# The cross attention's output projection as three products of high and low halves

## The reference

```
def memory_cross_attention(h, m, wq, wk, wv, wo):
    ...
    p = jax.nn.softmax(l, axis=-1).astype(vm.dtype)
    o = jnp.einsum('bhtm,bmhd->bthd', p, vm).reshape(Bn, T, W_X)
    return o @ wo                       # (256 x 256) @ (256 x 1024)
...
x = x + memory_cross_attention(rms_norm(x, norm_x), rms_norm(mem, mem_norm), wq_x, wk_x, wv_x, wo_x)
x = x + hier_moe(rms_norm(x, norm_moe), w_group, b_group, w_router, b_router, w1, w3, w2)
```

## Time and profile before

| | |
|---|---|
| time, median of 3 runs | 673.18 us (672.6 to 673.38) |
| time of the profiled execution | 671.9 us |
| its span, first to last instruction | 670.0 us |
| mean granted PE clock | 0.889 |
| PE busy | 508.9 us (76%) |
| DVE, ACT busy | 205.6 us, 144.5 us |
| DMA | 244.21 MB, 364 GB/s over the span |
| cross attention's output projection, first product to xo3 | 223.5 to 231.3 us |
| first expert product | 240.2 us |

### The profile page before, as it was taken

The page is one execution under the profiler, slowest core; times in us unless marked ns, Lnnn a source line. Parts: engine busy times, 40 slices in busy tenths (PEclk is TensorE's granted clock), DMA queues, the critical chain, the costliest instruction groups (busy, mean ns, idle before and its releaser), DMA issues.

```text
span 670.0 us, 8811 instructions
## 1 busy us (share of the span) xinstructions
PE 508.9 (76%) x3810; PEld 321.5 (48%) x3810; DVE 205.6 (31%) x384; ACT 144.5 (22%) x253; POOL 15.5 (2%) x31
## 2 busy tenths in 40 slices
PE   8999999999999997968743736764483576347575
PEld 7999998999999642413311411331141123114121
DVE  5799565588857431100000100000010000001002
ACT  4764545354635421000000000000000000000002
POOL 1200010001001000000000000000000000000001
PEclk9999999999999999997766978886798879569879
DMA  9998236908798999999999999999999999999994
GB/s 301 388 354 304 77 126 199 374 4 291 251 382 301 421 392 425 429 425 428 427 426 431 425 429 427 425 429 427 429 424 430 427 428 427 425 431 424 425 410 172
DMA packets 48857, 244.21 MB, mean 364 GB/s; under 512 B 6096, under 2 KB 19888, under 8 KB 36912
## 3 DMA queue, kind: packets, MB, share of 16 engines
q1 hardware_dynamic: 48816, 243.62, 90.0%
HBM read 242.53 MB, written 4.22 MB: 368 GB/s over the span
## 4 chain that ended last, share of the span: by engine, by line
PE 53%; DMA 44%; issue 1%; DVE 1%; ACT 1%; POOL 0%; PEld 0%; SPq 0%; POOLq 0%; PEldq 0%; DVEq 0%
PE ps L755 16%; DMA slots_late<-in_w 14%; PE ps L1145 11%; DMA slots_own<-in_w 9%; PE ps L778 7%; DMA attn_data<-in_w 7%; PE ps L1150 6%; DMA slot_last<-in_w 5%; DMA slot_spare<-in_w 5%; DMA slot_mixed<-in_w 5%; PE ps L733 1%; PE ps L826 1%; PE ps L894 1%; PE ps L923 1%; PE ps L1260 1%; PE ps L1008 1%
## 5 line engine op out<-in xcount | busy, mean ns | idle before, releaser
L1145 PE MATMUL ps<-slots_late,x_sb 128*32 128x512 f32 x320 | 85.8, 672 | 36.5 <-DMA slots_late<-in_w 13.4
L1145 PE MATMUL ps<-attn_data,x_sb 128*32 128x512 f32 x160 | 65.0, 719 | 12.4 <-DMA slots_own<-in_w 12.4
L1912 DVE TENSOR_TENSOR slot_extra<-ps,slot_extra 128x512 f32<-128x512 f32 x8 | 5.5, 691 | 214.1 <-ACT slot_extra L1524 214.1
L1145 PE MATMUL ps<-slot_spare,x_sb 128*32 128x512 f32 x128 | 58.8, 658 | 14.7 <-DMA attn_data<-in_w 14.7
L1521 ACT ACTIVATE slot_extra<-ps 128x256 f32<-128x256 f32 x8 | 3.1, 383 | 302.1 <-PE ps L1218 302.1
L1145 PE MATMUL ps<-slots_own,x_sb 128*32 128x512 f32 x240 | 59.4, 691 | 10.3 <-DMA slot_spare<-in_w 3.9
L453 DVE TENSOR_TENSOR w_low<-slots_own,w_high 128x2048 fp32r<-128x2048 f32 (+1 forms) x31 | 62.4, 2014 | 14.9 <-ACT w_high L1330 14.8
L1150 PE MATMUL ps<-slots_own,slot_extra 128*32 128x512 f32 x192 | 48.2, 713 | 16.4 <-DMA slot_last<-in_w 8.2
L1150 PE MATMUL ps<-attn_data,slot_extra 128*32 128x512 f32 x112 | 45.3, 734 | 16.7 <-DMA slots_own<-in_w 16.7
L1330 ACT ACTIVATE w_high<-slots_own 128x2048 fp32r<-128x2048 f32 (+1 forms) x31 | 52.3, 1689 | 17.3 <-PE ps L778 10.8
L755 PE MATMUL ps<-h_high,w_high 128*128 128x256 f32 x224 | 55.4, 288 | 0.0
(11 more groups left out here) (272 smaller groups left out, 880.4 us busy)
## 6 DMA issues: line engine op xcount, KB each, us to landing
slots_own<-in_w SPq DMA_DIRECT2D x24, 2048.0 KB, 34.1
slots_late<-in_w SPq DMA_DIRECT2D x23, 2048.0 KB, 35.0
attn_data<-in_w SPq DMA_DIRECT2D x14, 2048.0 KB, 35.4
slot_last<-in_w SPq DMA_DIRECT2D x9, 2048.0 KB, 35.6
slots_own<-in_w_in SPq DMA_DIRECT2D x8, 2048.0 KB, 10.1
slot_spare<-in_w SPq DMA_DIRECT2D x8, 2048.0 KB, 36.0
slot_mixed<-in_w SPq DMA_DIRECT2D x7, 2048.0 KB, 34.6
attn_data<-in_w SPq DMA_DIRECT2D x6, 1024.0 KB, 9.3
```

The source lines that it names most:

```text
L1145: return pe.matmul(ps[SLOTS * e:SLOTS * e + SLOTS, 4 + matrix, :], xeT[:, k, SLOTS * e:SLOTS * e + SLOTS], w, start=(k == 0), stop=(k == K ...
```

## The change

`xo0` to `xo3` are made of three fp32r products for each of the two depth tiles: high by high, low by high (both with the weights' high half), high by low. That is 24 products of 128x512 where there were 8 in float32.

- ACT makes the high half of wo in three copies (128x1024, 128x512, 128x512), put between its exponentials and before the copy of `vm`. They are written over wv_x, so ACT waits for the split of `vm` first. DVE makes the low half in two subtractions of 128x1024, in place over wo_x.
- ACT's copies of `ox0` and `ox1` now write `ox_high`; DVE subtracts that from PSUM into `ox_low`, and only DVE's instruction frees the bank.
- `xo0` and `xo1` are computed together, depth by depth. PE begins both before the first product.
- Unit 10 has no early half; it is loaded whole when `xo3` is computed.

```diff
-EARLY_HALF = {8: 0, 9: 0, 10: 0, 11: 1}
+EARLY_HALF = {8: 0, 9: 0, 11: 1}
...
-                    for early in (10, 8, 9):
+                    for early in (8, 9):
...
+            def cross_products(i, o, k, low):
+                t, c = i // 2, slice(512 * (i % 2), 512 * (i % 2) + 512)
+                for x_ in (ox_high,) if low else (ox_high, ox_low):
+                    m = pe.matmul(o, x_[:, k, t * P:(t + 1) * P], wo_parts[:, low, k, c], ...
...
-            o = begin("xo0")
+            pe.wait_ge(wo_high_set, 3)
+            firsts = [begin(f"xo{i}") for i in range(2)]
             for k in range(2):
                 job_evacuated(pe, f"ox{k}")
-                m = pe.matmul(o, oxT[:, k, 0:P], wo[:, k, 0:512], start=(k == 0), stop=(k == 1))
-            end(m, "xo0")
-            rows("xo1", wo, oxT, (0,), 512, 512)
+                for i in range(2):
+                    cross_products(i, firsts[i], k, 0)
+            for k in range(2):
+                pe.wait_ge(wo_low_set, k + 1)
+                for i in range(2):
+                    m = cross_products(i, firsts[i], k, 1)
+                    if k:
+                        end(m, f"xo{i}")
...
+            weights_split(act, "vm")
+            act.activation(wo_parts[:, 0, 0, :], wo_raw[:, 0, :], ACT.Copy).then_inc(wo_high_set, 1)
             cross_exp(0)
             cross_exp(1)
+            act.activation(wo_parts[:, 0, 1, 0:512], wo_raw[:, 1, 0:512], ACT.Copy).then_inc(wo_high_set, 1)
             cross_exp(2)
             cross_exp(3)
             cross_copy(0)
+            act.activation(wo_parts[:, 0, 1, 512:], wo_raw[:, 1, 512:], ACT.Copy).then_inc(wo_high_set, 1)
             copy_job("vm", vm.rearrange("p a b -> p (a b)"))
...
             cross_normalise(3)
+            wo_low(0)
             cross_copy(3)
+            for c in range(2):
+                o = job_computed(dve, f"ox{c}")
+                dve.wait_ge(ox_high_set, c + 1)
+                evacuates(dve.tensor_tensor(ox_low[:, c, :], o[:, 0:T], ox_high[:, c, :].bitcast(F32), ALU.subtract),
+                          f"ox{c}")
+            wo_low(1)
```

More of the change, by code:

```diff
@@ L197, in decoder_layer @@
         slots_late = sb("slots_late", [P, 3, SLOT])
+        with ExitStack() as early:
+            assert CHUNK_SLOT[CHUNKS.index("vx_ox")] == 6
+            wo_parts = early.enter_context(nc.sbuf_tensor("wo_parts", [P, 2, 2, 1024], F32R))
         attn_data = sb("attn_data", [P, 2, SLOT])
@@ L221, in decoder_layer @@
         vb = slot_extra[:, 3072:4096].rearrange("p (a b) -> p a b", a=TT)
+        with ExitStack() as early:
+            ox_high = early.enter_context(nc.sbuf_tensor("ox_high", [P, 2, T], F32R))
         iqT = sb("iqT", [P, 2, T])
@@ L226, in decoder_layer @@
         iw = sb("iw", [P, TT, IDX_HEADS])
+        with ExitStack() as early:
+            ox_low = early.enter_context(nc.sbuf_tensor("ox_low", [P, 2, T], F32R))
         memory_kv_data = sb("memory_kv_data", [P, D])
@@ L275, in decoder_layer @@
         unpicked = score
-        oxT = iqT
         def flat(buf):
@@ L370, in decoder_layer @@
         ikw_in = sem("ikw_in")
+        wo_high_set, wo_low_set, ox_high_set = sem("wo_high_set"), sem("wo_low_set"), sem("ox_high_set")
         iw_turned, keys_set, iw_scaled = sem("iw_turned"), sem("keys_set"), sem("iw_scaled")
@@ L1028, in _ @@
             end(query_products(1, q1, range(6, KD), low=True), "qx1")
-            wo = chunk("vx_ox")[:, 2048:4096].rearrange("p (k n) -> p k n", k=2)
             job_evacuated(pe, "km")
@@ L1064, in _ @@
                 end(m, f"ox{c}")
-            chunk_landed(pe, "vx_ox")
             def turn_for_router(i):
@@ L1090, in route, with cross_out @@
                           stop=True).then_inc(logits_done, 1)
-            o = begin("xo0")
+            def cross_products(i, o, k, low):
+                t, c = i // 2, slice(512 * (i % 2), 512 * (i % 2) + 512)
+                for x_ in (ox_high,) if low else (ox_high, ox_low):
+                    m = pe.matmul(o, x_[:, k, t * P:(t + 1) * P], wo_parts[:, low, k, c],
+                                  start=(k == 0 and not low and x_ is ox_high), stop=(k == 1 and low == 1),
+                                  skip_group_check=True)
+                return m
+            def cross_out(i):
+                o = begin(f"xo{i}")
+                for low in range(2):
+                    for k in range(2):
+                        m = cross_products(i, o, k, low)
+                end(m, f"xo{i}")
+            pe.wait_ge(wo_high_set, 3)
+            firsts = [begin(f"xo{i}") for i in range(2)]
             for k in range(2):
                 job_evacuated(pe, f"ox{k}")
-                m = pe.matmul(o, oxT[:, k, 0:P], wo[:, k, 0:512], start=(k == 0), stop=(k == 1))
-            end(m, "xo0")
-            rows("xo1", wo, oxT, (0,), 512, 512)
+                for i in range(2):
+                    cross_products(i, firsts[i], k, 0)
+            for k in range(2):
+                pe.wait_ge(wo_low_set, k + 1)
+                for i in range(2):
+                    m = cross_products(i, firsts[i], k, 1)
+                    if k:
+                        end(m, f"xo{i}")
             pe.wait_ge(xexp_set, X_HEADS)
@@ L1101, in _ @@
             turn_for_router(0)
-            rows("xo2", wo, oxT, (1,), 0, 512)
+            cross_out(2)
             turn_for_router(1)
-            rows("xo3", wo, oxT, (1,), 512, 512)
+            cross_out(3)
             turn_for_router(2)
@@ L1491, in cross_copy @@
                 act.activation(xprobT[:, h].rearrange("p a b -> p (a b)"), ps[:, 6, :], ACT.Copy).then_inc(xpT_copied_a, 1)
+            wo_raw = chunk("vx_ox")[:, 2048:4096].rearrange("p (k n) -> p k n", k=2)
+            weights_split(act, "vm")
+            act.activation(wo_parts[:, 0, 0, :], wo_raw[:, 0, :], ACT.Copy).then_inc(wo_high_set, 1)
             cross_exp(0)
             cross_exp(1)
+            act.activation(wo_parts[:, 0, 1, 0:512], wo_raw[:, 1, 0:512], ACT.Copy).then_inc(wo_high_set, 1)
             cross_exp(2)
@@ L1500, in _ @@
             for c in range(2):
-                copy_job(f"ox{c}", oxT[:].rearrange("p a b -> p (a b)")[:, c * T:(c + 1) * T], lambda o: o[:, 0:T])
+                o = job_computed(act, f"ox{c}")
+                act.activation(ox_high[:, c, :], o[:, 0:T], ACT.Copy).then_inc(ox_high_set, 1)
             for i in range(4):
@@ L1812, in _, with wo_low @@
             cross_normalise(3)
-            cross_copy(3)
+            wo_raw = chunk("vx_ox")[:, 2048:4096].rearrange("p (k n) -> p k n", k=2)
+            def wo_low(k):
+                dve.wait_ge(wo_high_set, 1 + 2 * k)
+                dve.tensor_tensor(wo_parts[:, 1, k, :], wo_raw[:, k, :], wo_parts[:, 0, k, :].bitcast(F32),
+                                  ALU.subtract).then_inc(wo_low_set, 1)
+            wo_low(0)
+            cross_copy(3)
+            for c in range(2):
[4 more added lines that the diff above has]
+            wo_low(1)
             for i in range(4):
```

## The result

| | before | changed |
|---|---|---|
| time, median | 672.62 us (22 runs, 671.4 to 674.04) | 673.6 us (22 runs, 672.46 to 678.28) |
| ratio | | 1.0016, 95% interval 1.0008 to 1.0023 |
| time of the profiled execution | 671.9 us | 673.12 us |
| its span | 670.0 us | 671.3 us |

The change costs 1.08 us (0.5 to 1.5). That is inside the 0.2% named ahead, but with 22 runs on each side it can be told from no change. With more runs the median of before came down from 673.18 to 672.62, so the forecast 673.5 met 673.6 partly by that luck: its difference was +0.36, and set on the later median it would have given 673.0.

A forecast was written before the change was run, and what follows sets the result against it. The weight stream was taken to bound the kernel, its end moved only through its hole at 241 to 244 us. Own time 671.9 + 0.36 = 672.3, with the median 1.28 above the profiled run: 673.5 us, range 672.1 to 675.0.

The forecast's parts named there:

- The end hangs on unit 12's issue: SP's weight load at 241.31 us waits for PE's first expert product; later widens the stream's gap without limit.
- the line: PE and DVE path from ox through xo0 to xo3, router and gathering to the first expert product; forecast +0.36 us.
- the hole of the earlier trace: Weight stream at 241 to 244 us, before the change: 213 GB/s instead of 428, 1.5 us of transfer lost.
- The two waits: PE idle about 0.9 us before xo0's first product (ox1's bank) and again before the first transpose (xo0 done late).
- the hand-overs take some 0.03 and 0.06: Before xo0's first product: added to DVE's 0.41 subtraction after ACT's ox1 copy ends at 223.94, giving 224.44.
- The other term: PE's fp32r product of 128x512 in xo0 to xo3: 0.227 us each, bounds 0.213 to 0.246.
- What was covered: ACT's three copies of wo and DVE's two subtractions fit idle time: cost 0; the copies uncovered would cost 2.3 us.
- Rival 2: Slower: new ACT or DVE instructions aren't covered, exponentials and vm's copy slip 0.6 each, +1.2 us, 674.7; chance 0.10.
- Unit 10 whole: Weight stream: the half asked for at about 212.6 moves behind xo3; margin 0.7 us before running dry, cost 0.
- the lost time is taken back: A dry spell before unit 10 shortens the gap at 241 equally; cost 0 until the loss passes 1.9 us.
- Rival 1: Slower: weight loads at L1102 aren't covered, 4.1 us more, 677.7; decides from 0.27 us a product; chance 0.06.
- The 675.6 given for the rule: Trainium skill's rule on PE's weight loads: 128-column loads add 0.107 us each, 23 x 0.107 = 2.5 us.

The follow-up runs named there:

- the version with the low half first: Changed kernel with xo0 then xo1, and DVE's second subtraction on the weights put ahead of those on ox; ratios to before 0.9996 and 0.9991.
- the kernel with the filler: Kernel before with 16 float32 products of 128x128 more on PE between ox1 and xo0; ratio to before 1.0059, time +4.0 us.

## Why the prediction was right, and where its sum was off

*The end hangs on unit 12's issue.* Right. Where the line is later and no bytes are lost elsewhere, the time follows it about one for one: +0.83 gave +1.1 (0.5 to 1.5), +1.32 gave +0.9 (0.1 to 1.6), +3.57 gave +4.0 (3.1 to 4.8). Downward the stream gained 1.5 with a line of -2.28, as the hole of the earlier trace rows said, but a gain in time wasn't seen: lines of -0.87 and -2.28 gave times that can't be told from none. Nor was the form of the hole as forecast: it isn't deeper from 241 to 244 us, it lasts longer.

*The two waits.* Right in kind and place, 1.20 and 0.71 us where 0.9 each was forecast. Begun singly or later, the line falls by 1.07 or 0.61.

*The size.* Forecast +0.36 on the line, measured +0.83, less than half of it foreseen and just past the upper end of the forecast (0.04 to 0.80). That the time still came out at 673.6 for 673.5 is the luck with the median of before, told above. Laid beside the forecast's steps (with 0.13 added to each time of after, for the mark):

| step | forecast | measured | off by |
|---|---|---|---|
| first product | 224.44 | 224.72 | +0.28 |
| from there to xo0's addition | 2.70 | 2.81 | +0.11 |
| to the first transpose | 0.92 | 0.89 | -0.03 |
| two jobs, two transposes, to xo3's addition | 3.80 | 3.90 | +0.10 |
| sum | +0.36 | +0.82 | +0.46 |

The term that was mis-sized most is "the hand-overs take some 0.03 and 0.06": from DVE's end to an idle PE are 0.24 in the chain, where I had put 0.06, and DVE's own step was 0.10 later and longer than I had it. With `xo1` begun later the same hand-over was 0.04. An idle PE alone doesn't make it long: in the changed kernel's own trace PE stands idle for 0.81 before its first product of the gathering, and from DVE's end to that are 0.04 too, in the chain and in the timeline:

```profile
239.66 0.04 issue
...
239.71 0.49 PE L1201 MATMUL ps<-iqT,xn 128*128 128x128 f32 x2 [0.81 <-DVE iqT L1937]
```

What goes with it in these kernels is the program behind the wait. Where the hand-over was 0.24 or 0.14, `job_evacuated("ox0")`, one more wait, stands between the wait that DVE ends and the product. With `xo1` begun later, and in the wait of 0.40 for the weights' low half, nothing stands there, and it was 0.04. No run changed that alone, so the reason stays open. The other term is the product: 0.233 for 0.227, and 0.30 for the first step behind the idle PE; the chain has the six products of xo2 and of xo3 at 1.41 and 1.39, where 1.36 was forecast, and the first four transposes, behind the second wait, at 0.63 instead of 0.44, most of which the addition of xo3 gives back, 0.04 behind the products instead of 0.20. The product stayed inside its bounds (0.213 to 0.246). The hand-over had none, and so the sum came out where only the end of the products' bounds had put it (+0.80).

*What was covered.* ACT's copies, DVE's subtractions: cost nothing, as forecast. Rival 2 needed their cover gone; with it partly gone the line lost 0.49.

*Unit 10 whole.* Cost 0.3 us at most, shown by itself. The reason that I gave for the case of a dry spell, "the lost time is taken back", looks too generous: of 2.4 us lost there, 1.3 stayed lost by the stream and the ratios, where by that reason it would have been some 0.5. The errors don't exclude the smaller value. It didn't come to that.

*Rival 1, uncovered weight loads.* Refuted. 0.233 a product with a load of 0.19 each is 0.02 above the 0.213 that 512 columns take at 2.4 GHz, and far below the 0.27 from which it would have decided. The Trainium skill (TensorE: Matmul & The Clock Gate, "The mechanism") has a load overlap with products only in another row group. In this trace loads over all 128 rows lay beside products over all 128 rows, so that sentence isn't borne out for this form. The same section also lets a load go ahead that targets a background weight buffer, which the prediction left out; the trace agrees with that as far as it can show it. The 675.6 given for the rule is 673.5 + 2.5 = 676.0 by the forecast's own terms.

*What stays open.* One execution of the changed kernel took 678.28 us. The lower granted clock at the end that explains the 677.59 with ACT's copies first would fit, but there is no trace of it. Nor is it settled whether the version with the low half first beats before by a few tenths.

## What to carry to other kernels

Where a long stream of DMA sets the end, look for its one hole, and price an edit by how it moves the issue that closes the hole: later cost about the full amount here; earlier filled the hole and no more, and bought no time that these runs could tell from none. Splitting a float32 product into three faster ones gained 0.3 us a job on PE here and lost it all at the two ends, because two jobs were begun together: the first product then waited for the second job's bank, and the first job was done only with the eleventh of twelve products. When operands of the new form are made on other engines, put the making into idle time, and give the hand-over back to PE bounds of its own in the sum: 0.04 to 0.24 us here.

## What the runs showed of the hardware

- An fp32r product of 128x512 took 0.233 us at a granted clock of 1.00, with a weight load of 0.19 for each beside it.
- From DVE's end to PE's product were 0.24 us in the changed kernel, 0.14 with the jobs one after the other, and 0.04 with `xo1` begun later; it was also 0.04 behind a PE that had been idle for 0.81.
- Over a pause of PE of some three microseconds near the end the granted clock stayed at 1.00 in the changed kernel's trace and fell to 0.50 in one of another kernel (ACT's copies first). The 128x512 products of the down projections then started 0.85 us apart instead of 0.43.
- A float32 product of 128x128 stands as two records: 16 products took 3.77 us, 0.24 each, in the kernel with the filler.
- After a dry spell the stream isn't full at once: with unit 12 issued at 242.01, 243 to 244 us moved 229 GB/s and 244 to 245 us 328 (the issue's data were flowing from about 243), against 427 later.
